# Layer 0's attention: its twenty-two modulation fills stand in steps 0 to 19, 31 and 32 instead of steps 1 to 22

## What is computed

```python
mod = (silu_c @ lp["w_mod"] + lp["b_mod"])[:, None, :]       # w_mod: 1024 x 6144, for each layer
...
o_mla = blocked_attend(q_mla, ...)      # 8 heads, 512 keys; context queries see 256 keys
o_gqa = blocked_attend(q_gqa, ...)      # 8 heads
o_four = fourier_mix(proj[..., FOUR_START:GATE_START])
x = x + gt1 * merge_branches(o_mla, o_gqa, o_four, proj[..., GATE_START:], lp)
```

## Time and profile before

| what | value |
|---|---|
| median of three runs | 1933.93 us |
| the profiled execution: its own time | 1933.26 us |
| its span in the trace | 1931.4 us |
| outside the span | 1.86 us |
| PE busy | 1870.8 us, 97% |
| DVE busy | 1143.9 us, 59% |
| ACT busy | 929.3 us, 48% |
| mean granted clock of TensorE | 0.994 |

### The profile page before, as it was taken

The page is one execution under the profiler, slowest core; times in us unless marked ns, Lnnn a source line. Parts: engine busy times, 40 slices in busy tenths (PEclk is TensorE's granted clock), DMA queues, the critical chain, the costliest instruction groups (busy, mean ns, idle before and its releaser), DMA issues.

```text
span 1931.4 us, 30701 instructions
## 1 busy us (share of the span) xinstructions
PE 1870.8 (97%) x11823; PEld 1564.7 (81%) x11823; DVE 1143.9 (59%) x1754; ACT 929.3 (48%) x1417; POOL 195.4 (10%) x191
## 2 busy tenths in 40 slices
PE   6999999999999999999999999999999999999998
PEld 3875556888878888888875699999989878899996
DVE  4326567333355555523536666677745578799887
ACT  3237556322234333311436655455534656487783
POOL 4000001000011322210100000023301000100000
PEclk8999999999999999999999999999999999999999
DMA  8435672433332232333355057645557442544443
GB/s 300 127 112 175 201 250 71 100 94 97 93 106 88 87 108 87 109 99 98 109 169 164 1 127 191 188 137 190 187 178 227 142 143 88 174 148 141 150 134 109
DMA packets 235460, 265.32 MB, mean 137 GB/s; under 512 B 6598, under 2 KB 175920, under 8 KB 235360
## 3 DMA queue, kind: packets, MB, share of 16 engines
q1 hardware_dynamic: 230464, 249.32, 41.6%
q0 software_dynamic: 4448, 13.49, 2.2%
q10 hardware_dynamic: 448, 1.12, 0.2%
HBM read 262.81 MB, written 1.10 MB: 137 GB/s over the span
## 4 chain that ended last, share of the span: by engine, by line
PE 87%; DVE 8%; ACT 3%; issue 1%; DMA 1%; SPq 0%; DVEq 0%; ACTq 0%
PE bank L492 23%; PE bank L493 23%; PE bank L494 23%; PE bank L748 3%; PE bank L769 2%; PE bank L756 2%; PE bank L486 2%; PE bank L539 2%; PE bank L603 2%; DVE weights_fine L1954 1%; PE bank L1030 1%; DMA region<-in_w_mod 1%; ACT weights_coarse L1217 1%; PE bank L571 1%; PE bank L995 1%
## 5 line engine op out<-in xcount | busy, mean ns | idle before, releaser
L1954 DVE TENSOR_TENSOR weights_fine<-region,weights_coarse 128x2048 fp32r<-128x2048 f32 (+2 forms) x181 | 417.7, 2308 | 341.4 <-ACT weights_coarse L1217 340.5
L1217 ACT CAST weights_coarse<-region 128x2048 fp32r<-128x2048 f32 (+3 forms) x185 | 355.1, 1919 | 342.1 <-PE bank L494 321.1
L492 PE MATMUL bank<-normed_coarse,weights_coarse 128*128 128x256 f32 (+1 forms) x1104 | 368.7, 334 | 1.5 <-DVE normed_fine L2108 0.8
L493 PE MATMUL bank<-normed_fine,weights_coarse 128*128 128x256 f32 (+1 forms) x1104 | 368.4, 334 | 0.0
L494 PE MATMUL bank<-normed_coarse,weights_fine 128*128 128x256 f32 (+1 forms) x1104 | 368.4, 334 | 0.0
L492 PEld LDWEIGHTS bank<-normed_coarse,weights_coarse 128*128 128x128 f32 x1104 | 209.7, 190 | 22.5 <-issue 1.9
L494 PEld LDWEIGHTS bank<-normed_coarse,weights_fine 128*128 128x128 f32 x1104 | 209.7, 190 | 20.6
L493 PEld LDWEIGHTS bank<-normed_fine,weights_coarse 128*128 128x128 f32 x1104 | 209.7, 190 | 20.3
L492 PE MATMUL bank<-x_turned_coarse,weights_coarse 128*128 128x256 f32 x616 | 177.9, 289 | 5.6 <-DVE weights_fine L1954 4.2
L494 PE MATMUL bank<-x_turned_coarse,weights_fine 128*128 128x256 f32 x616 | 175.7, 285 | 0.0
L493 PE MATMUL bank<-x_turned_fine,weights_coarse 128*128 128x256 f32 x616 | 175.6, 285 | 0.0
(11 more groups left out here) (303 smaller groups left out, 3475.0 us busy)
## 6 DMA issues: line engine op xcount, KB each, us to landing
region<-in_w_mod SPq DMA_DIRECT2D x48, 1024.0 KB, 5.4
region<-in_w_up SPq DMA_DIRECT2D x44, 1024.0 KB, 5.1
region<-in_w_in_c SPq DMA_DIRECT2D x30, 1024.0 KB, 5.2
region<-in_w_in_ab SPq DMA_DIRECT2D x20, 1024.0 KB, 5.3
region<-in_w_in SPq DMA_DIRECT2D x32, 512.0 KB, 4.9
region<-in_w_down SPq DMA_DIRECT2D x16, 1024.0 KB, 5.0
region<-in_w_in SPq DMA_DIRECT2D x14, 1024.0 KB, 5.2
region<-in_w_in SPq DMA_DIRECT2D x16, 384.0 KB, 3.5
```

Of the source, the lines that this page charges most:

```text
L492: nc.tensor.matmul(o, sc, mc, start=first, stop=False)
L493: nc.tensor.matmul(o, sc, mf, start=False, stop=False)
L1217: nc.scalar.copy(w_co[:, p, 0:size], raw_w[:, s, 0:size]).then_inc(coarse_ready, 1)
L1954: nc.vector.tensor_tensor(w_fi[:, p, 0:size], raw_w[:, s, 0:size], w_co[:, p, 0:size].bitcast(F32), ALU.subtract).then_inc(fine_ready, 1)
```

## The change

Three constants change, and with them the places of the same pieces of work. `MOD_FILLS` was 1 to 22 and becomes 0 to 19, 31 and 32, again twenty-two steps. `MOD_TURN` goes from 23 to 33 and `MOD_GATES` from 32 to 33. The unused argument `doubles` goes away, and the `elif` of `closing` becomes `if`, since turn and gates now stand in the same step. Nothing is added or left out: as many fills, `mod_turn`s, loads and DVE copies as before. Since a `mod_turn` precedes each first half, the turns move from the odd steps 1, 3, ..., 21 and 23 to the even steps 0, 2, ..., 18, and to 31 and 33.

```diff
-MOD_DOUBLE, MOD_LAST, MOD_TURN, MOD_GATES = (), 22, 23, 32
-MOD_FILLS = range(1, MOD_LAST + 1)
+MOD_TURN, MOD_GATES = 33, 33
+MOD_FILLS = (*range(20), 31, 32)
...
                 def closing(p):
                     if p == MOD_TURN:
                         mod_turn()
-                    elif p == MOD_GATES:
+                    if p == MOD_GATES:
                         gate_transposes(list(u.reads))
...
                     if p is None:
                         split(SLOT, 3)
-                    elif l == 0 and p == MOD_TURN:
-                        mod_turn()
-                    elif l == 0 and p == MOD_GATES:
-                        skip()
+                    elif l == 0:
+                        if p == MOD_TURN:
+                            mod_turn()
+                        if p == MOD_GATES:
+                            skip()
...
-                    if p in doubles:
-                        fill()
...
-                    if closing and p <= pairs:
+                    if closing and p <= pairs + 1:
                         closing(p)
...
                     if p == MOD_TURN:
                         mod_turned(turn_unit())
-                    elif p == MOD_GATES:
+                    if p == MOD_GATES:
                         other_gains(list(u.reads))
```

More of the change, by code:

```diff
@@ L728, in closing, with heads_loop @@
                         mod_turn()
-                    elif p == MOD_GATES:
+                    if p == MOD_GATES:
                         gate_transposes(list(u.reads))
                 heads_loop(16 * items_of(l), score, value, pr, prT, keys_of, exp_done, mod_half, MOD_FILLS if l == 0 else (), sums_t,
-                           MOD_DOUBLE if l == 0 else (), None if l else closing)
-            def heads_loop(heads, score, value, p_sb, pT_sb, keys_of, scores_read, fill, fills, sums, doubles=(), closing=None):
+                           None if l else closing)
+            def heads_loop(heads, score, value, p_sb, pT_sb, keys_of, scores_read, fill, fills, sums, closing=None):
                 base = seen[scores_read].n
@@ L1473, in closing, with heads_loop @@
                         split(SLOT, 3)
-                    elif l == 0 and p == MOD_TURN:
-                        mod_turn()
-                    elif l == 0 and p == MOD_GATES:
-                        skip()
+                    elif l == 0:
[3 more added lines that the diff above has]
+                            skip()
                 heads_loop(16 * items_of(l), pr, prT, lambda i: 512 if i < 32 else 256, None, mod_half,
-                           MOD_FILLS if l == 0 else (), after, True, MOD_DOUBLE if l == 0 else (), closing)
-            def heads_loop(heads, p_sb, pT_sb, keys_of, s_in, fill, fills, after, scaled=False, doubles=(), closing=None):
+                           MOD_FILLS if l == 0 else (), after, True, closing)
+            def heads_loop(heads, p_sb, pT_sb, keys_of, s_in, fill, fills, after, scaled=False, closing=None):
                 made, pairs, depth = [], heads // 2, p_sb.shape[1]
@@ L2288, in closing, with heads_loop @@
                         mod_turned(turn_unit())
-                    elif p == MOD_GATES:
+                    if p == MOD_GATES:
                         other_gains(list(u.reads))
                 heads_loop(16 * items_of(l), lambda i: 512 if i < 32 else 256, o_raw, sums_t, None,
-                           mod_half, MOD_FILLS if l == 0 else (), after, True, MOD_DOUBLE if l == 0 else (), None if l else closing)
-            def heads_loop(heads, keys_of, raw_o, sums, bias, fill, fills, after, scaled=False, doubles=(), closing=None):
+                           mod_half, MOD_FILLS if l == 0 else (), after, True, None if l else closing)
+            def heads_loop(heads, keys_of, raw_o, sums, bias, fill, fills, after, scaled=False, closing=None):
                 n0, copied = n_max[0], []
```

## The result

The changed kernel's median is 1936.74 us (1935.84 to 1938.95), that of the kernel before, measured beside it, 1933.99 us. The ratio is 1.0013 with a 95% interval of 1.0007 to 1.0019: 2.5 us slower, 1.4 to 3.7; the two medians themselves lie 2.75 us apart. The forecast was 1935.7 us (+1.8). In the terms of the forecast this is "the same" (within 0.2%), and measurably on the slow side, as forecast.

What follows compares the result with a forecast made beforehand. PE was taken to set the attention's pace with fills, and the chain score, maximum, exponential without them. -0.2 - 2.2 + 4.2 = +1.8 us on 1933.93 gave 1935.7 us, range 1932.0 to 1938.5.

Steps and rivals of the forecast that it cites:

- Step 0: Attention's first step gains a turn and a fill, partly in PE's idle time; net gain 0.2 us.
- Steps 1 to 19: Attention steps where turns move from odd to even steps and the sum of PE's work stays; zero.
- Steps 20 to 23: Attention steps losing three fills and two turns, 3.9 us of PE work; 2.2 us gained, as PE stops setting the pace.
- Load A: Weights split by ACT before fourier: issued only after step 31's fill, landing 6.3 us later, split 4.2 us later than before.
- Load B: Weight load issued behind load A after step 32's fill, its split needed only after fourier; costs nothing.
- The tail of step 33: Last attention step: turn and gates there delay fourier's start, a loss of 2.2 us lying beneath load A's 4.2.
- The sum: Whole kernel: -0.2 - 2.2 + 4.2 = +1.8 us, giving 1935.7 us.
- Rival 1: Load A lands in time and only the tail of step 33 decides: -0.2 us, 1933.7 us; chance 0.08.
- Rival 2: PE's clock falls to half around its waits before fourier, costing 1.65 or 5 us: 1937.4 or 1940.7 us; chance 0.12.
- the forecast's own sign: Stated in advance: the forecast would be wrong if the granted clock in 320 to 335 is under 1.
- Rival 3: Load A is complete only with load B, 11.5 us after issue, split 9.4 us late: 1940.9 us; chance 0.06.
- Rival 4: All PE work removed counts and the end is free: 4.2 us faster, 1929.7 us; chance 0.04.

Runs made afterwards that it cites:

- e1: The changed kernel run again with no edit, for a second profile; ratio 1.0017 (1.0008 to 1.0026) to the kernel before.
- e5: The kernel before, with load A held back until PE has done step 31's value products; ratio 1.0017 (1.0008 to 1.0026).
- e6: The kernel before, with load A held back until the gate transposes at the end of step 32; ratio 1.0034 (1.0021 to 1.0048).
- e8: The changed kernel with its two late fills in steps 30 and 31 instead of 31 and 32; ratio 0.9997 (0.9988 to 1.0006).
- e11: The changed kernel with no edit, for a third profile; 140.40 us from step 0's first scores to merge's first matmul.
- e9: As e8, but with the last turn in step 32 instead of 33; ratio 1.0001 (0.9992 to 1.0010).
- e7: The changed kernel with layer 0's split and fine part of load A moved from before fourier to before its fourth group; ratio 1.0010 (1.0001 to 1.0019).
- e3: The changed kernel with its two late fills in steps 29 and 30 instead of 31 and 32; ratio 1.0009 (1.0000 to 1.0018).
- e2: The changed kernel with fills in steps 0 to 21, last turn in step 22 and gates in step 32; ratio 0.9997 (0.9988 to 1.0006).

## Why the prediction was right, point by point

**Step 0 (-0.2).** Step 2 began 6.95 us after step 0 instead of 7.15. Right, and by the mechanism named: the idle time of the earlier trace rows was filled. Step 1's scores began 3.19 us behind step 0 with no idle time before them, which is 194.5 in the clock of the trace before (194.6 foretold).

**Steps 1 to 19 (zero).** Step 20 began 88.55 us behind step 0 in e1 and 88.81 before, so nothing beyond step 0's gain. In the first profile it was 89.72, for the wait of 1.10 us. The forecast had put no load's landing into its bounds here.

**Steps 20 to 23 (-2.2).** 10.02 us in e1 instead of 12.36: -2.34. It is not the 3.9 us of PE work that went; the earlier trace rows had said that PE does not set the pace without fills. Steps 24 to 30 took 17.66 us instead of 17.45: 0.2 us given back, a term that the sum did not have.

**Load A (4.2, from landing after 6.3).** It took 6.35 us from issue to the split, and 2.96 from the split to L810 (3.0 forecast). In the clock of the trace before, the split began at 316.23 + (126.80 - 124.91) = 318.12, with 2.39 us saved ahead of it (step 31 began 116.23 instead of 118.62 us behind step 0): 1.89 + 2.39 = 4.3 us late. e5 and e6 show that this cost stands by itself, microsecond for microsecond once the low clock's part is taken off, and e8 that it shrinks as the load goes out earlier. One detail of the forecast was off: ACT idled 5.2 to 5.4 us before the split, not "about 4"; the sum does not use that number. Load B cost nothing: the next split on ACT begins 1.86 us behind `merge`'s start, before and after.

**The tail of step 33 (2.2, beneath).** L800 began 126.46 us behind step 0 in the first profile, 125.25 in e1, and 125.82 before. So in e1 it is 0.57 us earlier, where -2.39 was saved: some 1.8 us lost there, a little less than 2.2, and it lay beneath the load's wait, as PE idled 2.59 us behind it. In e8 PE still waited 0.31 us for ACT before L810, with the load the last thing that ACT's split waited for; the tail's cost is next to it.

**The sum.** -0.26 - 2.34 + 0.21 + 4.28 = 1.9 us, as e1's stretch has it. But e1 is the one profile of three with neither the wait before step 18's fill nor a low clock. The mean of the three stretches is 2.5 us over 137.95, and the whole kernel is 2.5 us slower (1.4 to 3.7). So the mechanism and its terms were right, and what the forecast lacked is what comes on top in some executions: 1.1 us for a late weight load, 0.6 us for the clock. That these make up the 0.6 us between 1.9 and 2.5 is likely, but not shown: three profiles are few.

The forecast also read that PE runs without a gap through `merge` once the attention is over. That was not so before: fourier's third L812 waits 0.67 us for DVE. It did no harm to the sum, as the same wait is 0.73 us after.

**The rivals.** Rival 1 (load A in time) is out for the change: three profiles show ACT waiting 5.2 to 5.4 us for the DMA. Rival 2 (the clock) is no rival but an addition: in one of three profiles of the changed kernel (e11) the clock fell behind the wait before L810, at a cost of 0.6 us where the forecast had priced 1.65. By the forecast's own sign, a granted clock under 1 in 320 to 335, that profile speaks against it and the other two do not. The argument against this rival had been a wait of some 2.3 us, shorter than the 2.48 and 2.80 of the earlier trace rows; it came out at 2.45 to 2.59 us. Rival 3 (A and B together) is out: it took 6.35 us with B issued from 317.69 on behind it, where 8.4 would have been needed. The Trainium skill (DMA: Bandwidth & Descriptors, Queues, rings and completion order) says that each DMA engine consumes descriptors in the order of the ring; the trace agrees, as A was not held up by B. Rival 4 is out: the four steps took 10.02 us, not 8.5, and the load was not there.

No arrangement tried beats the kernel before by what five rounds can tell. e8 has the shortest stretch, 0.9 us under 137.95, and a ratio of 0.9997 (0.9988 to 1.0006), which can neither show nor rule out a gain of that size.

## What to carry to other kernels

A filler that is moved to the end of a stage, where its engine has idle time, takes its buffers along. With a ring of two slots the next stage's first load can go out only behind it, and the time from issue to use (here 6.35 us) must fit between the filler and the first reader, or behind everything that the reader's engine does in order. Try the place one step earlier: here it cost little pace and took 2.8 us off the load's lateness, though even so the kernel was not measurably faster than before. And compare two executions of one kernel from the first instruction that the change can touch; here 2.45 of 5.8 us lay ahead of it.

## What was not expected of the hardware

Executions differ by 2 to 3 us outside the stretch. Step 0 began at 191.32 and 191.36 us in the two profiles of the kernel before, at 193.77, 192.70 and 191.23 in the three of the change, at 190.52 in e9, and at 193.37 to 193.67 in the other seven. From `merge`'s start to the end it took 1601.9 to 1604.2 us. The stretch of the kernel before agreed to 0.01 us in between, that of the changed kernel only to 1.2. Why the parts outside differ is open.

The granted clock fell to half (1.2 GHz) after short waits, but not after each. After 2.58 and 2.59 us of idle time before L810 it stayed full (the first profile of the change, e1); after 2.45 (e11), 2.83 (e5) and 2.01 us (e7) it fell, and within the 6.41 us of e6. In e3 it fell behind waits of 1.31 and 0.41 us. In e2 no single wait was over 0.95 us, and the same waits left it full in the kernel before. It stayed low for some 3.5 us in e2, e7 and e11, and for about 7 in e3, e5 and e6. The Trainium skill (TensorE: Matmul & The Clock Gate, Why this matters for your kernels) names idle gaps between bursts; e5, e6, e7 and e11 agree. What decides between a wait with a fall and one without is not shown.

One load of 1 MB took 7.7 us to land, where the same load took 5.1 in e1, and made PE wait 1.10 us. That came in two of the eight profiles of kernels whose fills stand in steps 0 to 19 (the first of the change, and e7, with 7.7 and 1.15 us), always at step 18's fill, and in none of the five profiles with the fills of before. Whether the new place of the fills makes it likelier, two cases can't tell.
